# Dilated tail, Fourier gate, GpSimd sums in halves, four first transfers and four reorderings in a two-block transformer kernel

## What is computed

```
x = x + 0.5 * swiglu(rms_norm(x, g1), w_in1, w_out1)                 # ffn1
y_b = dilated_attention(q, k, v)                                      # 12 heads, softmax over lse of 3 groups
merged = sigmoid(g_a) * (y_a @ w_proj_rwkv) + sigmoid(g_b) * (y_b @ w_proj_attn)
x = x + merged @ w_out;  x = x + 0.5 * swiglu(rms_norm(x, g2), ...)   # mix_out, ffn2
for l in (0, 1):
    gm, gd, gf = split(sigmoid(h @ w_gates))
    y = gm * (mlstm(h) @ w_ml) + gd * (diff_attn(h) @ w_da) + gf * (fft2(h @ w_fn).real @ w_fnp)
    x = x + mod * (y @ w_out);  x = x + mod * swiglu(...)             # l{l}_ffn
```

## Time and profile before

| | us |
|---|---|
| median of 3 runs | 3039.05 |
| lowest and highest | 3038.08 to 3042.87 |
| the profiled execution | 3039.35 |
| its span, first to last instruction | 3037.50 |
| outside the span | 1.85 |

### The profile page before, as it was taken

The page is one execution under the profiler, slowest core; times in us unless marked ns, Lnnn a source line. Parts: engine busy times, 40 slices in busy tenths (PEclk is TensorE's granted clock), DMA queues, the critical chain, the costliest instruction groups (busy, mean ns, idle before and its releaser), DMA issues.

```text
span 3037.5 us, 37659 instructions
## 1 busy us (share of the span) xinstructions
PE 2979.6 (98%) x15358; PEld 2249.3 (74%) x15358; DVE 1783.6 (59%) x2606; ACT 598.6 (20%) x1184; POOL 540.0 (18%) x214
## 2 busy tenths in 40 slices
PE   8999999999999999999999999999999999999998
PEld 4448898765458858886688878888888888768543
DVE  6994742657766556667853358777424602752574
ACT  2103222222121112103611131110021200510110
POOL 4330000023332101221021112211110001010332
PEclk9999999999999999999999999999999999999999
DMA  6663301355543302442021234444232143143453
GB/s 265 231 243 139 139 31 58 111 189 177 194 180 125 111 28 76 151 150 74 28 97 56 83 146 159 146 144 139 99 117 95 70 158 112 61 153 143 152 180 125
DMA packets 57115, 389.86 MB, mean 128 GB/s; under 512 B 9072, under 2 KB 23408, under 8 KB 36336
## 3 DMA queue, kind: packets, MB, share of 16 engines
q1 hardware_dynamic: 52592, 383.27, 35.1%
q10 hardware_dynamic: 4352, 4.20, 0.7%
HBM read 373.53 MB, written 1.05 MB: 123 GB/s over the span
## 4 chain that ended last, share of the span: by engine, by line
PE 90%; DVE 7%; ACT 2%; issue 1%; DMA 0%; DVEq 0%; SPq 0%; ACTq 0%
PE bank L1140 88%; PE bank L1143 1%; DVE weights L3200 1%; DVE arena L3529 0%; DVE factors L3213 0%; DVE factors L3108 0%; ACT h_T L2295 0%; DVE weights L3203 0%; DVE h_T L3302 0%; DVE arena L3230 0%; PE bank L1147 0%; DVE arena L3047 0%; DVE masks L3999 0%; DVE arena L3897 0%; DVE arena L3563 0%
## 5 line engine op out<-in xcount | busy, mean ns | idle before, releaser
L1140 PE MATMUL bank<-h_T,weights 128*128 128x256 f32 (+1 forms) x3184 | 778.6, 397 | 8.8 <-ACT h_T L2295 2.4
L1140 PEld LDWEIGHTS bank<-h_T,weights 128*128 128x128 f32 x3184 | 600.6, 191 | 140.8 <-issue 58.4
L2919 POOL TENSOR_TENSOR weights<-weights 128x1024 f32<-128x1024 f32 (+2 forms) x105 | 277.9, 2647 | 1268.3 <-DMA weights<-wide_slabs_dram 1170.4
L2930 POOL TENSOR_TENSOR factors<-weights 128x1024 f32<-128x1024 f32 (+2 forms) x105 | 264.2, 2516 | 1201.1 <-PE bank L1140 881.7
L1140 PE MATMUL bank<-arena,weights 128*128 128x256 f32 x1784 | 393.9, 379 | 2.5 <-DVE arena L3230 0.9
L1140 PEld LDWEIGHTS bank<-arena,weights 128*128 128x128 f32 x1784 | 337.8, 190 | 51.4 <-issue 1.8
L1140 PE MATMUL bank<-factors,weights 128*128 128x256 f32 x1432 | 323.9, 379 | 5.0 <-DVE arena L3230 3.9
L1140 PE MATMUL bank<-weights,h_T 128*128 128x256 f32 (+2 forms) x1000 | 323.6, 470 | 3.1 <-DMA weights<-wide_slabs_dram 2.2
L1140 PE MATMUL bank<-weights,factors 128*128 128x256 f32 (+1 forms) x960 | 313.8, 471 | 4.1 <-DVE factors L3213 1.8
L1140 PEld LDWEIGHTS bank<-factors,weights 128*128 128x128 f32 x1432 | 271.6, 190 | 43.3 <-DVE arena L3230 5.1
L1140 PEld LDWEIGHTS bank<-weights,h_T 128*128 128x128 f32 x1000 | 190.3, 191 | 116.6 <-issue 89.8
(11 more groups left out here) (392 smaller groups left out, 2688.0 us busy)
## 6 DMA issues: line engine op xcount, KB each, us to landing
weights<-wide_slabs_dram SPq DMA_DIRECT2D x143, 2048.0 KB, 7.8
arena<-wide_slabs_dram SPq DMA_DIRECT2D x61, 512.0 KB, 4.1
weights<-down_slabs_dram SPq DMA_DIRECT2D x8, 1408.0 KB, 5.8
merged_T<-arena SPq DMA_DIRECT2D x240, 32.0 KB, 1.9
merged_T<-wide_slabs_dram SPq DMA_DIRECT2D x15, 512.0 KB, 4.4
x_T<-wide_slabs_dram SPq DMA_DIRECT2D x11, 512.0 KB, 9.3
arena<-arena ACTq DMA_DIRECT2D x16, 256.0 KB, 10.0
weights<-wide_slabs_dram SPq DMA_DIRECT2D x3, 1024.0 KB, 5.0
```

The lines of the kernel that those rows point to most:

```text
L1140: return mm(out, lhsT, rhs, start=start, stop=stop, skip_group_check=True)
L2919: nc.gpsimd.tensor_tensor(b[2], b[2], b[3], ALU.add).then_inc(S["first_sums"], 1)
L2930: nc.gpsimd.tensor_tensor(e, b[2], b[0], ALU.subtract).then_inc(S["first_sums"], 1)
```

## The change

It consists of these parts, named by letters here and below.

- **A, start:** slab 0 comes in four transfers of a block each, in the order b0, b2, b3, b1. P1 waits for b0, POOL's S1 for b2 and b3, P2 for b1. ACT scales blocks 11 and 12 before it squares any.
- **B, down stage's first sums:** S3 and S4 of down slab 0 stand between the last two `half_hid`s in `half_up`.
- **C, row sums:** `mod_window(1)` runs after C22 of its unit.
- **D, group norms of layer 0:** S4 stands right behind S3; the scaling is two instructions of 2048 columns; PE transposes groups 0 to 3 ahead of the unit's P7 and 4 to 7 after it; C22 is joined after DVE has taken four groups.
- **E, dilated tail:** the eight k steps of tile 0 of `dil_gate1` run in steps 12 to 15 of the loop, five, one, one and one.
- **F, Fourier gate:** in layer 0, P1 of `fn_gate0` (moved to bank 3) stands ahead of channels 4 to 7; in layer 1, tile 0 of `fn_gate0` stands ahead of the transform over channels. The wait for all of `fn_halves` comes later on PE, that for `fn_out` later on ACT. The first unit of `l1_fn` runs P2 ahead of P5.
- **G, halves:** each of POOL's 210 sums is two instructions of half the columns.

```diff
-            units[name, j] = Unit(name, j, len(units), wide[0], 3 * ((len(run) + (stage == "ffn_down")) % 2))
+            units[name, j] = Unit(name, j, len(units), wide[0], 3 * ((len(run) + (stage == "ffn_down" or "fn_gate0" in stages)) % 2))
...
             if j == 0:
-                self.order = ("P1", "P5", "P2", "P6", "P3", "P7", "P4")
+                self.order = ("P1", "P2", "P5", "P6", "P3", "P7", "P4") if self.kind == "fn" else ("P1", "P5", "P2", "P6", "P3", "P7", "P4")
...
+                    if (st.name, j) == FIRST_UNIT:
+                        for quarter in (0, 2, 3, 1):
+                            part = slice(quarter * words // 4, (quarter + 1) * words // 4)
+                            sp.dma_start(ring[:, part], view[:, part]).then_inc(S[("first_block", "landed0", "first_pair", "first_pair")[quarter]], 16)
+                        return
...
+            def gate1_begins(ks):
+                st = ST["dil_gate1"]
+                if 0 in ks:
+                    arrived(st, 0)
+                    t.wait("probs_in", 2)
+                for k in ks:
+                    last = matmul(bank[0][:, 0:T], wtile(st, 0, k), H1[:, k], start=k == 0, stop=k == KT - 1)
+                if KT - 1 in ks:
+                    last.then_inc(S["tile_done"], 1)
             for h in range(16):
...
                 if 3 <= h < 15:
                     dil_turn(h - 3)
+                if h >= 12:
+                    gate1_begins((range(0, 5), (5,), (6,), (7,))[h - 12])
                 if h >= 4:
                     dil_values(h - 4)
-            t.wait("probs_in", 2)
             t.wait("pv_out", 2)
-            gate("dil", 1, [("act_out", ST["dil_gate0"].act_end)], part=(0, 3))
+            gate("dil", 1, [("act_out", ST["dil_gate0"].act_end)], part=(1, 3))
...
-                        (gate0, "P5"): ml_banks_free, (proj0, "P1"): lambda: token_outputs_back(t, transpose, Y_ML, qtiles, 8),
+                        (gate0, "P5"): ml_banks_free,
+                        (gate0, "P7"): lambda: token_outputs_back(t, transpose, Y_ML, qtiles, range(4)),
+                        (proj0, "P1"): lambda: token_outputs_back(t, transpose, Y_ML, qtiles, range(4, 8)),
...
                     channels(range(4))
                     end_units(run)
+                    product(RUNS[3][0], "P1")
                     pe.wait_ge(S["act_out"], ST[p + "fn"].act_end)
                     channels(range(4, KT))
...
+                if la == 1:
+                    project(ST[p + "fn_gate0"], lambda k: H2[:, k, 0:nq], nq, part=(0, 1), frees=[("half_joined", HALF_JOIN["C21", (p + "fn", 0)])])
...
-                t.wait("fn_halves", 4)
...
+                if stage is None:
+                    even_block(norm, "11", 7)
+                    even_block(norm, "12", 2)
+                    for which in ("11", "12", "22", "21"):
+                        token_square(norm, which)
+                    return
...
-                nc.gpsimd.tensor_tensor(b[2], b[2], b[3], ALU.add).then_inc(S["first_sums"], 1)
-                pool.wait_ge(S["first_sums"], u.weights("S1"))
+                cols = b[2].shape[-1]
+                halves = slice(0, cols // 2), slice(cols // 2, cols)
+                for half in halves:
+                    nc.gpsimd.tensor_tensor(b[2][:, half], b[2][:, half], b[3][:, half], ALU.add).then_inc(S["first_sums"], 1)
+                pool.wait_ge(S["first_sums"], u.first_halves("S1"))
...
-                nc.gpsimd.tensor_tensor(e, b[2], b[0], ALU.subtract).then_inc(S["first_sums"], 1)
+                for half in halves:
+                    nc.gpsimd.tensor_tensor(e[:, half], b[2][:, half], b[0][:, half], ALU.subtract).then_inc(S["first_sums"], 1)
...
                     half_hid(up, j, 0, norm, False)
+                    if j == ST[up].slabs - 1:
+                        block_sum((down, 0), "S3")
+                        block_sum((down, 0), "S4")
                     half_hid(up, j, 1, norm, True)
...
-                        if la == 0:
+                        if la == 0 and i != 1:
                             mod_window(i)
...
-                    unit(key, inside=rows_and_modulation(i))
+                    unit(key, inside=rows_and_modulation(i), after=(lambda: mod_window(1)) if (la, i) == (0, 1) else None)
...
+                def outputs_scaled(base, roots, groups):
+
+                    n = D // groups
+                    y = A[:, base:base + qtiles * D].rearrange("p (q g n) -> p q g n", q=qtiles, g=groups)
+                    r = roots.rearrange("p (q g) -> p q g", q=qtiles)
+                    for part in ((slice(0, groups // 2), slice(groups // 2, groups)) if la == 0 else (slice(0, groups),)):
+                        t.out(tt(y[:, :, part], y[:, :, part], bc(r[:, :, part], 3, n), mul), "dve_for_pe")
...
                 if la == 0:
                     block_sum(run[0], "S3")
+                    block_sum(run[0], "S4")
```

More of the change, by code:

```diff
@@ L3284, in unit @@
                         inside()
+                if after:
+                    after()
             def say(name):
@@ L3802, in _ @@
                 if la == 0:
-                    block_sum(run[0], "S4")
                     join(run[0], "C11")
-                yv = A[:, Y_ML:Y_ML + qtiles * D].rearrange("p (u n) -> p u n", n=256)
-                t.out(tt(yv, yv, bc(rt, 2, 256), mul), "dve_for_pe")
+                outputs_scaled(Y_ML, rt, 4)
                 bT = tiles(A, 0, KT, 2 * T)
                 if la == 0:
-                    for which in ("C12", "C22"):
-                        join(run[0], which)
+                    join(run[0], "C12")
                 t.wait("act_for_dve")
                 for k in range(KT):
+                    if la == 0 and k == 4:
+                        join(run[0], "C22")
                     t.wait("pe_for_dve")
@@ L3893, in _ @@
                 if la == 0:
-                    block_sum(run[0], "S4")
                     join(run[0], "C11")
-                yv = A[:, 12288:12288 + qtiles * D].rearrange("p (u n) -> p u n", n=P)
-                t.out(tt(yv, yv, bc(rt, 2, P), mul), "dve_for_pe")
+                outputs_scaled(12288, rt, 8)
                 if la == 0:
-                    for which in ("C12", "C22"):
-                        join(run[0], which)
+                    join(run[0], "C12")
                 for k in range(KT):
+                    if la == 0 and k == 4:
+                        join(run[0], "C22")
                     t.wait("pe_for_dve")
```

73 lines of the change are left out of this document (47 added, 26 removed).

## The result

The changed kernel takes 3017.83 us (median of 4, 3016.73 to 3018.12), the kernel before 3039.47 (4 runs, 3038.08 to 3042.87). The ratio is 0.9926, with a 95% interval of 0.9914 to 0.9938: 21.6 us faster, where 18 were forecast. Timed again later beside other kernels, the same file had a median of 3021.81 us (5 runs, 3018.31 to 3022.24) and a ratio of 0.9938 (0.9926 to 0.9951). All nine executions together have a median of 3018.3.

The account below looks back on a forecast made before the run. The prediction took PE's matmul queue, with 57.9 us idle in short holes, as the bound. Parts A to G summed as 1.1 + 2.4 + 2.4 + 1.5 + 6.8 + 3.5 + 0.3 = 18.0 us, forecasting 3021.0 us, range 3013 to 3031.

Parts of the forecast that it names:

- A: First unit: b3 lands at 11.0, POOL starts earlier, and P7 gains 1.1 us, bounds 0.3 and 2.4.
- B: Down stages: S3 earlier gains 0.5 us in ffn1, 1.0 in ffn2, 0.9 in l1_ffn; 2.4 in all.
- C: Row sums: PE's 2.38 us wait for C12 and C22 goes, gaining 2.4 us, from 1.9.
- D: Group norms: 1.2 us gained in the mLSTM, net 0.3 in the attention after a new 1.1 us wait.
- E: Dilated tail: ten records fill the 2.51 us hole, the clock stays at 0.99, gaining 6.8 us.
- F: Fourier stages: gains of 2.1 us in layer 0, 0.8 in layer 1, 0.6 in l1_fn; 3.5 in all.
- G: GpSimd sums elsewhere: two 1 us stops replace one of 2 for busy DVE; 0.3 us, from -2 to 1.5.
- The bound: Whole kernel: a queue of matmuls on PE, with 57.9 us idle in some sixty short holes, plus clock lost behind the longest.
- Rival (1): Dilated tail: the clock falls all the same, the gain there is 3.5 us, total 3024.3; chance 0.17.
- rival (4): Start: the four transfers land with one another, 1.1 us less gain, 3022.1; counted within the forecast's 0.62.
- Rival (2): ffn1, attention's norm, Fourier: new waits for DVE's S3 and S4 take gains back, 3025.8; chance 0.17.
- Rival (3): GpSimd's 210 sums: each pair of halves holds the port 0.20 us longer, up to 3063; chance 0.04.

Follow-up runs that it names:

- e2: The kernel before with only the dilated-tail change (tile 0 of dil_gate1 in steps 12 to 15): 3032.38 us, ratio 0.9981.
- e4: The changed kernel with step 12 of the dilated tail left empty, its five k steps moved to step 13: 3025.54 us, ratio 0.9956.
- e9: The changed kernel with norm sums 128 columns wide and dummy products in PE's waits, two behind ffn1, three behind ffn2: 3014.19 us, ratio 0.9919.
- e12: The changed kernel with slab 0 in one transfer again and ScalarE's squares ahead of its scalings: 3022.80 us, ratio 0.9942.
- e3: The kernel before with only GpSimd's sums cut into halves: 3035.73 us, ratio 0.9988.
- e1: The changed kernel with each of GpSimd's sums one whole instruction again: 3026.55 us, ratio 0.9959.
- e8: The changed kernel with the matmuls that sum squares for the layer norms 128 columns wide in place of 2: 3016.49 us, ratio 0.9925.
- e5: The changed kernel with GpSimd's two sums of the very first unit whole, all others halves: 3020.04 us, ratio 0.9935.
- e11: The changed kernel timed again with no edit: 3021.81 us, ratio 0.9938.
- e6: The changed kernel with layer 0's head outputs scaled by four instructions in place of two: 3022.12 us, ratio 0.9945.
- e10: As e9, with whole GpSimd sums in the first unit and its S4 ahead of two additions: 3013.38 us, ratio 0.9915.

## Why the prediction was right, and where it was not

The time, 3017.8 us, lies in the stated range of 3013 to 3031, 3.2 us below the forecast of 3021.0. In the traces the gain is 21.4 us where 18.0 were written: A to F gave 0.4 more, G's own places 1.8 more, and 1.3 came by luck, from a seam that no part touches.

**The bound** was read rightly: the gain came out of PE's holes (13.9 us) and for the most part of the rest (7.5) out of the clock behind them.

**E** was right in each term: 0.23 us of hole left (0.4 written), clock 1.00, 6.84 us of gain (6.8 written, though its own figures, 630.06 less 623.1, make 7.0), and again 6.8 in e2. Rival (1) didn't come; e4 shows that it would have, had the hole stayed. In e4 the clock falls behind the hole and in e9 it stays up where the holes are filled. The rule on idle gaps (Trainium skill, TensorE: Matmul & The Clock Gate, section HAM oscillation) agrees in direction only: it asks for longer gaps than these, and here 2.51 us in e4, and 1.74 us behind ffn2 in some of the traces, were enough.

**C** (2.4, measured 2.6) and **F** (2.1, 0.8, 0.6; measured 2.1, 0.9, 0.5) hold. So does **D** in the mLSTM, 1.2. In the attention the new wait was forecast at 1.1 us and is 1.13, and the net of 0.3 is 0.0. The row from which that wait was costed is this one of the kernel before, the scaling in one instruction:

```profile
1516.87 6.05 DVE L3897 TENSOR_TENSOR arena<-arena,small 128x4096 f32<-128x4096 f32 x1
```

**B** was right in ffn2 and l1_ffn and too low in ffn1 (0.5 written, 1.1 measured). The mechanism was the one written: the wait at slab 1 grew from 0.51 to 1.10 us. The term that was mis-sized is the collision at slab 2, where I took 1.0 us less wait on a hole of 1.07 and then half of it away for the slab behind.

**A** was wrong by a rate. "b3 at 11.0" came from dividing 5 us by four; b0 came when it was forecast (8.63, 8.5 written), but b2 took 2.1 us behind it in place of 1.3, so b3 landed at 12.02 and POOL's first half began at 12.09. That is the lower bound of A, "if the last transfer's landing is what it was", and in effect rival (4), to which I gave no chance of its own; but the transfers landed in a row, not with one another. P1 did start earlier, at 11.05 (9.8 written), since it waited 0.96 us for ACT's scaled block, and its eight records ran at 1.2 GHz, 3.75 us, where e12's took 1.99. The 0.5 us by which the first unit is faster there need no part A: e3, halves alone, has 0.8 and e12 is 0.2 ahead without A. With whole sums A does gain: e1's P7 starts at 19.54, 1.76 us ahead of before, and 0.8 of it stay. There S3 takes 1.22 us in place of 3.25, because POOL's next sum starts behind it, at 18.36, when slab 1 has landed. So A and the halves gain at the same S3, and together they give 0.5.

**G** is the step that failed: 0.3 us written, 2 to 3.5 alone, 5 to 6 in company. The argument was that a DVE that is never idle meets two stops of 1 us in place of one of 2. It doesn't meet two of 1 us: at the cut DVE gets its turn, its stop is only what is left of the half under way, and the other half waits for it. At the end of mix_out, before and then after:

```profile
674.44 1.68 DVE L3121 TENSOR_TENSOR factors<-factors,arena 128x512 f32<-128x512 f32 x1
...
676.88 2.00 DVE L3123 TENSOR_TENSOR factors<-factors,arena 128x512 f32<-128x512 f32 x1
```

```profile
664.27 3.04 POOL L2982 TENSOR_TENSOR factors<-weights 128x512 f32<-128x512 f32 x2 [4.57 <-PE bank L1153]
...
665.49 0.69 DVE L3177 TENSOR_TENSOR factors<-factors,arena 128x512 f32<-128x512 f32 x1
...
666.94 0.92 DVE L3179 TENSOR_TENSOR factors<-factors,arena 128x512 f32<-128x512 f32 x1
```

Beside the 0.69 us of the undisturbed instruction, stops of 1.0 and 1.3 us became none and 0.2; a third instruction, undisturbed before (L3126, 0.69 us), now stops for 0.7. POOL's pair takes 3.04 us in place of 2.50, for which nobody waits; and PE is 1.6 us earlier behind them. Over the whole kernel DVE's busy time shows it: 1783.6 us before and 1784.0 in e1, with whole sums, against 1713.4 in e3 and 1715.7 in after, with halves. The second error is that I priced G by itself. D's new wait was costed with halves, so part of their worth was hidden in its term; with whole sums the wait is 2.2 us longer, and 3.3 with its clock. The same holds of B in ffn1, where e3 gains 1.0 us by halves alone.

**Rival (2)**, gains given back, was right as a mechanism and small: 0.6 at ffn1's slab 1 and the new wait in the attention, and in e8 1.25 behind the seam at 1787. **Rival (3)** has its price confirmed and its place refuted: POOL's pair of halves takes 2.50 us where a whole sum took 2.35, 0.15 more (0.20 written), and no place in the comparison shows a loss by it; what halves lose at P7 of the first unit (1.3 us, 0.5 of which stay, by e5) comes of DVE's factor sums between them, as the prediction of A says. (The 23 ns that G took from the earlier trace rows are the difference of two means with stops in them.)

**The clock** outside the tail was in the range only as "one stretch less elsewhere", and that is what came: the seam at 889 was at 0.50 in the trace of before and at 1.00 in that of after, behind the same wait of 1.74 us, for 1.3 us that no part of the change made: luck. That the later five executions have a median of 3021.81, 0.8 us from the forecast, is luck too: by the inference at e11 three of them lost 3.5 us to a late landing, which the prediction doesn't know.

## What to carry to other kernels

Set two traces of the same instruction list record against record before explaining a total: the table of parts above is worth more than any timing of 0.1%. Where two engines block each other by the instruction, price the cut together with the waits that stand next to it, on both engines: the other one's cut (G) gained 5 us, one's own (e6) lost 3. Where a matmul engine waits between stages, give it something to do, and try it wide; here ten useful records gained 6.8 us in the tail, of which the records' own time is 2.15; ten dummy ones and sums of 128 columns in place of 2 gained 4.0 us by the traces of after and e9, luck in two of the seams not excluded. Before cutting a transfer into pieces, read when each piece lands: here the four pieces took 1.1 us longer than the whole.

## What the runs showed of the hardware

- The granted clock fell to 0.50 behind holes of 1.2 to 3.3 us, and behind the same hole (1.74 us at the seam of ffn2) in some kernels' traces and not in others'. Executions of one file differ by up to 6.3 us (e2); those of the two kernels with no seam at 0.50 in the trace by 2.4 (e9) and 0.9 us (e10), those of e8 by 1.4.
- One and the same transfer of 2 MB was used 9.6, 10.5 or 12 us after its issue, in different kernels' traces, and 1.5 us of landing became 3.1 us of time, since the clock was at 0.50 behind the wait that it lengthens.
- Four transfers of 512 KB landed one after another, at 8.63, 10.73, 12.02 and 13.30 us, where one of 2 MB landed at 12.20; from 8.0 to 9.5 us 221 GB/s were moved in place of 437.
- Two seams begin with 24 records of 2 columns, for which PE is counted busy: they were at 0.50 in 10 of 11 traces (1781) and in 11 of 11 (2194). With 128 columns in the same records both were at 1.00 in 3 of 3, and the records at 2194 took 2.84 us in place of 2.74.
- VectorE holds GpSimd up as much as the other way round: a pair of GpSimd's halves took 2.5 us alone and 6.1 to 6.6 us beside two VectorE instructions of 2048 columns, and one VectorE sum of 1024 columns took 1.22 us alone and 3.25 beside a whole sum of GpSimd's.
